# A block with a gated-delta mixer and two expert layers: the decay setup of the first mixer rewritten, and one quarter of a modulation moved behind the output projection

## The reference

```python
gc = jnp.cumsum(chunks_s(g), axis=-1)                    # log decay, summed along a chunk
diff = gc[..., :, None] - gc[..., None, :]
decay = jnp.where(lower, jnp.exp(jnp.where(lower, diff, 0.0)), 0.0)
a_mat = jnp.where(strict, jnp.einsum('nbhid,nbhjd->nbhij', kb, kc) * decay, 0.0)
t_inv = lax.linalg.triangular_solve(eye + a_mat, ...)     # unit lower triangular
attn_intra = jnp.where(lower, jnp.einsum('nbhid,nbhjd->nbhij', qc, kc) * decay, 0.0)
q_dec = qc * jnp.exp(gc)[..., None]
```

## Time and profile before

| | us |
|---|---|
| median of three runs (lowest, highest) | 1646.04 (1641.35, 1655.28) |
| the profiled execution, its own time | 1649.46 |
| its span | 1647.7 |
| input projection ends | 129.6 |
| last diagonal input ready (`at_ready` 8) | 151.9 |
| DVE's loop starts, its result is out | 162.9, 188.7 |
| first join on TensorE | 189.5 |
| scan starts | 208.1 |
| output projection starts | 243.4 |

### The profile page before, as it was taken

One profiled execution on the slowest core, in us unless ns is written; L12 is line 12 of the kernel. 1 busy time (PEld: TensorE's weight loads), 2 busy tenths in 40 slices (PEclk: granted clock), 3 DMA queues, 4 the chain that ended last, 5 costly groups with the idle time before them and its releaser, 6 DMA issues.

```text
span 1647.7 us, 21985 instructions
## 1 busy us (share of the span) xinstructions
PE 1347.5 (82%) x9580; PEld 888.2 (54%) x9580; DVE 579.9 (35%) x1137; ACT 432.0 (26%) x647; POOL 218.2 (13%) x119
## 2 busy tenths in 40 slices
PE   6999999999999987567667668999967766665678
PEld 3787698999999952122122123999722212221227
DVE  4667735888257511011011012686201101100116
ACT  3345345444453220000000012584210000000005
POOL 0407322787420000000000000000000000000000
PEclk9999899999999998788788788999988878878889
DMA  9314443444555999999999999459899999999992
GB/s 401 140 73 168 194 175 146 175 183 141 198 198 216 363 413 426 428 426 425 430 427 426 426 427 411 166 204 356 312 426 426 428 428 425 428 427 427 426 411 104
DMA packets 52626, 528.45 MB, mean 321 GB/s; under 512 B 4784, under 2 KB 4912, under 8 KB 20144
## 3 DMA queue, kind: packets, MB, share of 16 engines
q1 hardware_dynamic: 51952, 525.22, 77.8%
q10 hardware_dynamic: 576, 1.79, 0.3%
HBM read 525.94 MB, written 1.05 MB: 320 GB/s over the span
## 4 chain that ended last, share of the span: by engine, by line
PE 55%; DMA 37%; DVE 3%; SPq 2%; ACT 2%; issue 1%; POOL 0%; DVEq 0%; ACTq 0%; POOLq 0%
PE bank L670 25%; PE bank L1293 9%; DMA ring<-in_w_gate 8%; DMA ring<-in_w_up 8%; DMA ring<-in_w_down 6%; DMA work<-in_w_down 6%; DMA work<-in_w_up 5%; PE bank L1313 4%; DMA work<-in_w_gate 4%; PE bank L1375 3%; PE bank L663 2%; PE bank L1443 2%; SPq L564 1%; PE bank L772 1%; PE bank L742 1%
## 5 line engine op out<-in xcount | busy, mean ns | idle before, releaser
L1293 PE MATMUL bank<-ring,work 128*32 128x512 f32 x1232 | 322.1, 734 | 135.6 <-DMA ring<-in_w_gate 69.4
L670 PE MATMUL bank<-work_rounded,ring_rounded 128*128 128x256 f32 (+1 forms) x2000 | 302.9, 286 | 2.3 <-DVE work_rounded L2077 1.3
L670 PEld LDWEIGHTS bank<-work_rounded,ring_rounded 128*128 128x128 f32 x2000 | 265.9, 188 | 9.9 <-issue 3.0
L670 PE MATMUL bank<-xn_rounded,ring_rounded 128*128 128x256 f32 (+1 forms) x1472 | 248.6, 285 | 1.1 <-DVE xn_rounded L2111 1.1
L1293 PEld LDWEIGHTS bank<-ring,work 128*32 128x32 f32 x1232 | 70.1, 130 | 311.4 <-issue 117.7
L670 PEld LDWEIGHTS bank<-xn_rounded,ring_rounded 128*128 128x128 f32 x1472 | 202.7, 188 | 5.6 <-issue 2.6
L2663 DVE TENSOR_TENSOR work<-work,bank 128x512 f32<-128x512 f32 x16 | 11.0, 688 | 548.3 <-PE bank L1293 548.3
L1977 POOL TENSOR_TENSOR ring_rounded<-ring,ring_rounded 128x2048 fp32r<-128x2048 f32 (+1 forms) x37 | 158.0, 4287 | 185.1 <-ACT ring_rounded L1516 185.1
L1293 PE MATMUL bank<-work 128*32 128x512 f32 x496 | 154.5, 672 | 34.0 <-DMA work<-in_w_gate 17.4
L2045 POOL TENSOR_TENSOR work<-work_rounded,work 128x128 f32<-128x128 f32 x32 | 12.2, 401 | 1060.9 <-PE bank L1350 727.4
L1516 ACT ACTIVATE ring_rounded<-ring 128x2048 fp32r<-128x2048 f32 (+1 forms) x76 | 133.0, 1795 | 51.7 <-PE bank L670 33.8
(11 more groups left out here) (338 smaller groups left out, 1736.7 us busy)
## 6 DMA issues: line engine op xcount, KB each, us to landing
ring<-in_dense SPq DMA_DIRECT2D x47, 2048.0 KB, 8.8
ring<-in_w_up SPq DMA_DIRECT2D x38, 2048.0 KB, 30.4
ring<-in_w_gate SPq DMA_DIRECT2D x36, 2048.0 KB, 30.0
ring<-in_w_down SPq DMA_DIRECT2D x34, 2048.0 KB, 28.8
work<-in_w_gate SPq DMA_DIRECT2D x16, 2048.0 KB, 22.8
work<-in_w_down SPq DMA_DIRECT2D x16, 2048.0 KB, 32.0
spare<-in_w_gate SPq DMA_DIRECT2D x8, 2048.0 KB, 28.9
work<-in_w_up SPq DMA_DIRECT2D x8, 2048.0 KB, 33.1
```

The costliest lines, as they stand in the source:

```text
L670: last = mm(out, rv(high_store[r][:, at:at + P]), rv(x[part][k]), start=opens and k == 0 and j == 0, stop=closes and k == n_k - 1 and j == 2)
L1293: ins = mm(out[slots(y), :], xg[:, k, slots(y)], expert_columns(w, at, 512), start=k == 0, stop=k == KT - 1)
```

## The change

1. Decay rows. Three small sets of products (12 in all, output 32 partitions wide) write the summed decays of both directions and beta transposed into bank 7; ACT copies them to SBUF (`rows_sb`). `decay_rows` and `beta_rows` then spread one row of them with products over 32 rows each, instead of 128. There are as many of them as before.
2. Exponents. Instead of DVE's `difference` and POOL's mask, `min(x, 0)` is formed as a Relu of the signed difference, with the column value as bias, one instruction per head, on ACT for pairs 0, 2, 4, 5, 6, 7, and on DVE for pairs 1 and 3; the exponential follows on ACT as before. The four attention matrices get a Relu pass of their own and are masked on POOL (multiplied by 0 or 1).
3. The diagonal blocks are first gathered into `packed` (copies on POOL, ACT and DVE), and then turned by one transpose over 128 partitions.
4. The product of query-key and attention decay moves from DVE to POOL, from a copy of the products that ACT makes (`qk_sb`).
5. Order: TensorE's first two modulation rows come ahead of `vtok`; ACT evicts the second one and the transposes only behind its last attention pass. ACT's exponential of the columns (`gexps`) comes later, and so does DVE's `begc`. The column additions of part 1 stand at steps 11, 14, 17, 20 of DVE's loop. `c_cols` moves, so that it no longer shares memory with the new rows.
6. Modulation chunks get four slots (1, 2, 0 and the spare one) instead of three.
7. The last quarter of part 2 is taken out of the stage: its row products take the place of two of the four idle products behind the output projection, its column products stand between the early and the late sums of squares, and DVE adds it behind its scaling.

The core of the diff, in the order of the file: plan, TensorE, ACT (from `def exponent`), POOL (from `pack(slice(0, 2), ...)`; the second loop there stands behind the four query and eight value products), DVE (from `exponent(1)`).

```diff
+USES = [("ada0", 4), ("kv", 8), ("q", 2), ("z", 2), ("u", 2), ("dft_w", 2), ("ada1", 2), ("vtok", 4), ("ktok", 4), ("dft_b", 4),
+        ("ada1b", 6), ("ada2", 1), ("dft_y", 2), ("ada2b", 5),
...
+                r = (1, 2, 0, SPARE_RING)[c]
...
+        def spread(b, group, x, r, h):
+            part = slice(32 * group, 32 * group + 32)
+            one = ident[part, 32 * group + r + h:32 * group + r + h + 1].to_broadcast([32, P])
+            return mm(bank[b][:, P * h:P * h + P], one, rows_sb[part, x], start=True, stop=True)
+        def decay_rows(n):
+            for h in range(HEADS):
+                for d in range(2):
+                    last = spread(row_bank[2 * n + d], d, d, 8 * token_of(n, d) + 4 * d, h)
+                    if h == HEADS - 1:
+                        signal(last, "g_rows")
...
+        key_products(0, 4)
+        key_products(1, 5)
+        pe.wait_ge(S["rows_sb"], 1)
         decay_rows(0)
...
+        pe.wait_ge(S["at_ready"], 4)
+        decay_rows(3)
+        pe.wait_ge(S["att_exp"], 1)
+        ada_rows(1, 0)
+        pe.wait_ge(S["att_exp"], 2)
+        ada_rows(1, 1)
+        token_major("vtok", vc, {0: ("at_ready", 6), 1: ("at_ready", 7)})
+        token_major("ktok", kc)
+        query_products(2, 6)
+        pe.wait_ge(S["at_ready"], 8)
+        query_products(3, 5)
...
         sum_squares(late)
-        idle_products(4)
-        ready = norm_input()
+        ada_rows(2, 3)
+        idle_products(2)
+        sum_squares(early)
+        ada_columns(2, 3)
+        ready = norm_input(late)
...
+        def exponent(out, e, sign, d, u):
+            for h in range(HEADS):
+                last = act.activation(out[:, h], bank[row_bank[e]][:, P * h:P * h + P], ACT.Relu,
+                                      bias=(gneg, gcol)[sign < 0][:, d, u, h:h + 1], scale=sign)
+            return last
...
+        for e in range(6):
+            decayed(e)
+            if e >= 4:
+                query_decay(e)
+                attention_decay(e)
+        decayed(6)
+        decayed(7)
+        ada_rows(1, (0,))
+        pack(slice(2, 4), 8)
+        query_decay(6)
+        attention_decay(6)
+        query_decay(7)
+        attention_decay(7)
+        signal(act.activation(gexps, gcs, ACT.Exp), "gc_exp")
+        ada_rows(1, (1,))
         for stage, tile in (("vtok", "vtok"), ("ktok", "ktok")):
...
+        pack(slice(0, 2), 4, range(4))
+        pack(slice(2, 4), 8, (2,))
+        for e in range(4):
+            pool.wait_ge(S["att_exp"], e + 1)
+            pool.tensor_tensor(attnT[:, e], attnT[:, e], heads(keep[:, e % 2]), ALU.mult).then_inc(S["att_masked"], 1)
...
+        for e in range(4):
+            pool.tensor_tensor(attnT[:, e], attnT[:, e], qk_sb[:, u - 2], ALU.mult).then_inc(S["att_ready"], 1)
...
+        exponent(1)
+        for e in range(0, 8, 2):
+            if e == 2:
+                exponent(3)
+            u, x, keys = by_keys(e)
+            before = signal(v.tensor_tensor(x, keys, x, ALU.mult), "dve_step")
+            u1, x1, keys1 = by_keys(e + 1)
...
-        for q in range(4):
-            part = slice(32 * q, 32 * q + 32)
-            last = v.transpose(blocks[part].rearrange("p (r c) -> p c r", r=32), flat_amat[part, part])
+        after(v.tensor_copy(packed[last_quarter, :, 2:4], amat[last_quarter, :, 2:4, :, last_quarter]))
+        dve.wait_ge(S["packed"], 1)
+        dve.wait_ge(S["packed_pool"], 2)
+        after(v.transpose(blocks.rearrange("p (r c) -> p c r", r=32), packed.rearrange("p d u h c -> p c (d u h)")))
...
-            if j in (9, 14, 18):
-                columns_added(1, (9, 14, 18).index(j) + 2)
+            if j in (11, 14, 17, 20):
+                columns_added(1, (11, 14, 17, 20).index(j) + 1)
```

More of the change, by code:

```diff
@@ L931, in _ @@
+        signal(last, "rate_mm")
+        for x, (m, columns) in enumerate(((cums[0], glog), (cums[1], glog), (ident, beta))):
+            for h in range(HEADS):
+                last = mm(bank[7][32 * h:32 * h + 32, P * x:P * x + P], columns.rearrange("p u c -> p (u c)"), m, start=True, stop=True)
+        signal(last, "rate_mm")
         key_products(0, 4)
         key_products(1, 5)
-        for n in (USE["dft_w"], USE["dft_w"] + 1):
-            released(pe, n)
-        rates = glog.rearrange("p u c -> p (u c)")
@@ L936, in _ @@
-        for i, m in enumerate((cums[0], cums[1], ones)):
-            last = mm(bank[7][:, 32 * i:32 * i + 32], m, rates, start=True, stop=True)
-        signal(last, "rate_mm")
+        pe.wait_ge(S["rows_sb"], 1)
         decay_rows(0)
-        for e in (1, 2, 3):
-            decay_rows(e)
         beta_rows(0)
-        decay_rows(4)
         pe.wait_ge(S["gate_cols"], 2)
-        decay_rows(5)
+        decay_rows(1)
+        beta_rows(1)
+        pe.wait_ge(S["decay"], 2)
+        decay_rows(2)
@@ L946, in _ @@
+        pe.wait_ge(S["decay"], 3)
+        key_products(2, 3)
+        pe.wait_ge(S["decay"], 4)
+        key_products(3, 6)
+        pe.wait_ge(S["at_ready"], 2)
         beta_rows(2)
[L947 to L950 removed]
         pe.wait_ge(S["at_ready"], 3)
[L952 to L953 removed]
+        beta_rows(3)
         pe.wait_ge(S["at_ready"], 4)
[L955 to L956 removed]
@@ L963, in _ @@
-        for m in range(2):
-            ada_step(1, m)
         for x in range(2):
@@ L1650, in ada_rows, with query_decay, pack @@
+        def query_decay(e):
+            signal(act.activation(qd[:, e - 4], by_head(bank[row_bank[e]]), ACT.Exp), "qd_exp")
+        def pack(us, ready):
+            act.wait_ge(S["at_ready"], ready)
+            for q in range(2):
+                part = slice(32 * q, 32 * q + 32)
+                last = act.activation(packed[part, :, us], amat[part, :, us, :, part], ACT.Copy)
+            signal(last, "packed")
         def ada_rows(part, ms):
@@ L1657, in ada_rows @@
                     full(ada_use(USE, part, 2 * m - 2))
-                free(act.activation(ada_row[part][:, m % 2], bank[n % BANKS][:], ACT.Copy), n)
-        ada_rows(1, (0, 1))
+                row = late_row if (part, m) == (2, 3) else ada_row[part][:, m % 2]
+                free(act.activation(row, bank[n % BANKS][:], ACT.Copy), n)
+        act.wait_ge(S["gate_cols"], 2)
+        for e in range(6):
[13 more added lines that the diff above has]
+        ada_rows(1, (1,))
+        for stage, tile in (("vtok", "vtok"), ("ktok", "ktok")):
+            for u in range(4):
+                to_sbuf(stage, u, wk(tile, 512, 512 * u))
+        act.wait_ge(S["qk_mm"], 2)
+        for u in range(2):
+            signal(act.activation(qk_sb[:, u], by_head(bank[(6, 5)[u]]), ACT.Copy), "qk_sb")
         for x in range(4):
```

188 lines of the change are left out of this document (88 added, 100 removed).

## The result

The changed kernel takes 1660.09 us (median of 14 runs, 1651.64 to 1664.73), the kernel before 1646.66 (14 runs, 1641.35 to 1655.28): 13.4 us more by the medians. The ratio, which is that of the means, is 1.0077 (95%: 1.0062 to 1.0092), or 12.7 us. The prediction was 1660.6 with a range of 1644 to 1668, and "within 1%" at 0.71.

What follows compares the result with a forecast made beforehand. Two chains were taken to end together, DVE at 188.7 us and TensorE at 189.5. Join 13, clock 1 and moved quarter 0.5 summed to +14.5 us: 1660.6 against the median 1646.04, range 1644 to 1668.

Steps and rivals of the forecast that it cites:

- fourth `vtok`: TensorE's fourth value transpose, needing bank 1 emptied by ACT, would start at 161.5 us, with TensorE idle 5 us.
- step 11, third column addition: Step 11 of DVE's loop, where DVE frees bank 2 for TensorE, would fall at about 184 us instead of 167.
- first join: Behind DVE's result at 201.5 and TensorE's list, the first join would start at 202.5 us, 13 later.
- The narrow products and the first exponent: Start of decay setup: narrow products 0.8 us, first pair of decay rows 0.9; first exponent at 136.4 instead of 134.9.
- 32 rows cost as much as 128: Rival on the decay-row products: no saving from fewer rows, adding 0.7 us to the start; no separate chance given.
- ScalarE's pass: On ACT, four Relu of 0.26 us, a wait and an exponential of 0.52 make a pass of 1.7 us.
- The port: POOL's products reading SBUF beside DVE's loop lengthen the loop by 17.7 us, bounds 0 to 20.4; chance 0.6.
- TensorE's wait: At the third column product TensorE would wait some 9 us for DVE to free bank 2.
- Clock: After TensorE's 9 us gap some columns may run at half speed: 1 us taken, 0 to 3.
- Moved quarter: Its column products ahead of the late sums of squares push those by 0.5 us, bounds 0 to 1.
- No sharing: Rival: DVE's loop runs undisturbed beside POOL, TensorE's list ends at 194.5, +5.0; about 1652 us; chance 0.27.
- Faster: Rival: ScalarE's queue is shorter and the port does not matter; join at 184 at best, half gives 1643; chance 0.1.

Runs made afterwards that it cites:

- z1_best: Kernel before plus the gather and single transpose, the last modulation quarter moved, and the eight value products on ScalarE: 1643.4 us, ratio 0.9981 to the kernel before.
- x1: Changed kernel with GpSimd's mask, query, value and attention products replaced by memsets, so results are wrong: ratio 1.0012 to the kernel before.
- y2: Kernel before with only the last modulation quarter moved behind the output projection: ratio 1.0000 to the kernel before.
- x4: Changed kernel with the eight value products on ScalarE instead of GpSimd, computation whole: ratio 1.0040 to the kernel before.
- x8: Changed kernel with ScalarE's reading of the second modulation quarter and four value-transpose copies put ahead of the last exponentials: ratio 1.0076 to the kernel before.

## Why the prediction was right

Its steps, from the start of the Fourier products (its own times less 129.56, the measured ones less 125.17):

| step | predicted | measured |
|---|---|---|
| first exponent | 6.8 | 7.7 |
| pass on ScalarE | 1.7 | 1.70 |
| eighth exponential done | 23.8 | 24.6 |
| `at_ready` 8 | 25.5 | 26.4 |
| loop starts | 28.9 | 30.1 |
| fourth `vtok` | 31.9 | 33.1 |
| step 11, third column addition | 54.4 | 54.0 |
| stretch of the loop by GpSimd | 17.7 | 15.4 |
| VectorE's first result | 71.9 | 71.3 |
| first join | 72.9 | 74.3 |

*The narrow products and the first exponent.* Right in kind, 0.9 late in small pieces: behind ScalarE's eviction (127.68) the rate products started only at 128.04 and took 0.76 where 0.6 was taken, and the key products took 1.98 and not 1.8. Two row groups do overlap: 48 spreading instructions took 2.83 us, 0.059 each against 0.115 for full ones. The rival "32 rows cost as much as 128" falls.

*ScalarE's pass.* 1.70 as predicted. The Trainium skill's figure ("ScalarE: Activation LUTs", "What ACT_TABLE_LOAD costs"), 0.29 us for 128 columns with a column operand, agrees with the trace of z1_best: twelve of its scaled copies start at 169.66 and the next instruction at 173.17, so 0.29 each. By it the ten passes would have been 1.3 us longer than by my 0.26 a Relu, but the wait that I had put on top is inside the measured 1.70.

*The port.* The size came from the earlier trace rows, rows of other shapes. 15.4 us (41.24 - 25.87, the latter confirmed by x1) against 17.7. The count of 18 products was right, and GpSimd's products beside the loop were a little longer than taken. What was mis-sized is what each costs: the prediction took off 0.15 us of overhead. The rows show that while GpSimd reads, VectorE passes **one instruction per GpSimd instruction** and so takes its length instead of its own. The 18 stretched instructions lasted 21.5 us and take 6.1 us in x1: 15.4, the whole of it, 0.34 off for each. Where GpSimd stops for want of an operand, two or more pass (156.77 to 157.85, four at normal length).

*TensorE's wait.* Predicted some 9 us, measured 5.04. The prediction's own terms give 7 to 8: 15.6 us of work from 161.5 ends at 177.1, and the bank is free at 184 to 185. The list then restarted 1.1 later than predicted and took 16.2. Part of that fit is luck: the five transposes that it begins with were priced at 4.5 and took 4.3, but at a clock of 0.50; six of them took 2.84 before. VectorE's addition came when predicted, so this moved nothing at the end.

*A slip in the sum.* Step 11 at 184 and 17.5 us of work behind it make 201.5, not 202.5. The 13 us at the join need the stretch of 17.7 in full (158.5 + 8.6 + 17.7 = 184.8), with which VectorE's result would be at 202.3 and not at 201.5. The total is loose by up to 1 us here.

*Clock.* 1 us was taken (0 to 3), 2.3 measured behind the wait. With it the join is 14.3 later than before, where the prediction had 13 and 1.

*Moved quarter.* +0.5 was taken, 0.1 measured in y2. The DMA wait of 0.98 us did go.

*The rivals.* No sharing: refuted by x1 and x4. The time it gave, 1652, can be set beside x1, where nothing is stretched: the list ended 66.6 after the start (predicted 64.9), and the ratio 1.0012 is 1648.6, 3 us less than 1652. But in x1's trace the join is 6.5 later than before, which bears the rival's +5.0 and some clock out; the ratio does not follow the trace there, and x1 computes wrong values, so it settles the sharing and not the rival's price. Faster: ScalarE's last attention pass would have had to end 5 us earlier; x8 shows that even a list restarted at 28.4 gains nothing beside the port. At the join and the quarter together 14.4 us were measured against 14.5 predicted, but with errors that cancelled: the stretch was 2.3 smaller, the starts 1.1 later and the clock 1.3 more. The mechanism was right; that the median (1660.09) fell within 1 us of 1660.6 is luck.

What stays open: outside the stage the executions differ by some microseconds either way. From the stage's end to 422 us the difference to before stays at 10.7; then TensorE's granted clock is lower in the changed kernel. Busy time by stretch, before and after, at the same times (the changed kernel is there 10.7 us or more behind in its work):

```profile
570.00:600.00 30.00, 29.43 (x241) 19.79 (x240) 8.45 (x41) 7.52 (x17) 0.76 (x2) 0.94 0.93 366
570.00:600.00 30.00, 29.43 (x212) 29.04 (x212) 8.04 (x41) 6.91 (x16) 0.76 (x2) 0.83 0.77 301
```

Set 11 us apart, to compare the same work, the clock is 1.00 from 540 to 570 before and 0.93 from 551 to 581 after. By the marks of ScalarE's table loads the part from 411 to 580 us of the kernel before takes between 167.7 and 173.0 us in the thirteen traces, with no order by kernel. The changed kernel has the longest (172.95, before 168.73), and 1.8 us come back later. Whether its mean clock over all runs (0.887 to 0.894, before 0.892 to 0.899) follows from the longer waits in the stage or adds to the time by itself was not tried.

## What to carry to other kernels

Before you delay or keep work on GpSimd, list what VectorE does in that time: if its instructions take two operands from SBUF and GpSimd reads SBUF, count one GpSimd instruction's whole length in place of its own for every VectorE instruction, however short, and look for another engine or for writes only. When an engine's chain is shortened so that it starts earlier, check what it now runs beside. And when a wait is taken away from a queue, look at the next instruction behind it: two of my experiments moved one copy and met the same wait one bank later.

## What the runs showed of the hardware

- VectorE instructions of 31 elements take 0.98 us beside GpSimd products of 1.00, and 1.25 beside its masks of 1.26; alone 0.19. GpSimd itself is hardly slowed (1.11 instead of 1.00 for a value product), but when VectorE has the port first, a 0.6 us copy on GpSimd took 2.75 while four of VectorE's products ran for 2.48.
- A 4-column VectorE instruction costs 0.16 or 4.26 us by whether it starts 1.6 us before or 0.4 us behind the start of a GpSimd instruction of 4.6 us. The two profiled executions fell on different sides, and all that follows moved by up to 4.4 us; of the thirteen traces only those of the kernel before and of x8_order3 start the stage at 129, the others at 125 to 126.
- Spreading products over 32 rows in separate row groups ran at 0.059 us an instruction, half of the full ones' 0.115; the 24 instructions of the narrow products (output 32 partitions wide) took 0.86 us together.
- Behind the waits of 6.09 and 5.04 us the granted clock was 0.50, and the second wait so cost 7.3 us, not 5.0; the same work took 3.75 and 2.52 us instead of 2.05 and 1.92.
